# Layer one's operand stored in blocks of 16 tokens, high and low parts in turn, and its 512 columns walked in runs of eight

## The reference, cut to what matters

```python
hs = jnp.concatenate([meta, x], axis=1)          # 16 + 256 tokens
h = rmsnorm(x, gain)
zin = h @ w_in                                    # 2048 x 12288
q, k, v, g_attn, u, g_pool, m_attn, m_pool = jnp.split(zin, cuts, axis=-1)
...                                               # attention over q, k, v; pooled means of u
merged = sigmoid(m_attn) * y_attn + sigmoid(m_pool) * y_pool
return x + merged @ w_out
```

## Time and profile before

| | us |
|---|---|
| median of 3 runs | 2767.71 (2766.85 to 2773.09) |
| the profiled execution | 2766.82 |
| its span in the profile | 2765.1 |
| TensorE busy in the span | 2746.5 (99%) |
| VectorE busy | 1907.3 (69%) |
| ScalarE busy | 1353.2 (49%) |

### The profile page before, as it was taken

The page is one execution under the profiler, slowest core; times in us unless marked ns, Lnnn a source line. Parts: engine busy times, 40 slices in busy tenths (PEclk is TensorE's granted clock), DMA queues, the critical chain, the costliest instruction groups (busy, mean ns, idle before and its releaser), DMA issues.

```text
span 2765.1 us, 39573 instructions
## 1 busy us (share of the span) xinstructions
PE 2746.5 (99%) x16256; PEld 2443.9 (88%) x16256; DVE 1907.3 (69%) x2553; ACT 1353.2 (49%) x1741; POOL 59.4 (2%) x103
## 2 busy tenths in 40 slices
PE   9999999999999999999999999999999999999998
PEld 8899888888888889999999988888888888888887
DVE  7655567778866657888888885566666655666556
ACT  5434654447444436656565643543354443444444
POOL 0000210000000000000000000000000000000000
PEclk9999999999999999999999999999999999999999
DMA  7444445465555454444444445554355455555554
GB/s 273 183 193 158 151 169 197 184 251 184 208 178 211 180 186 168 153 153 153 151 154 151 169 168 212 183 191 163 141 206 197 184 192 204 202 194 191 195 193 152
DMA packets 72852, 506.64 MB, mean 183 GB/s; under 512 B 8384, under 2 KB 8512, under 8 KB 12896
## 3 DMA queue, kind: packets, MB, share of 16 engines
q1 hardware_dynamic: 71136, 497.77, 48.6%
q0 software_dynamic: 1104, 5.90, 0.6%
q10 hardware_dynamic: 432, 0.45, 0.0%
HBM read 499.89 MB, written 2.10 MB: 182 GB/s over the span
## 4 chain that ended last, share of the span: by engine, by line
PE 95%; DVE 3%; ACT 1%; issue 1%; DMA 1%; SPq 0%; DVEq 0%; ACTq 0%
PE double L1399 88%; PE bank L1399 6%; PE bank L1402 1%; DVE wlo L2117 1%; ACT whi L1775 0%; DVE AA L2123 0%; DMA vec<-in_vec 0%; DMA raw<-in_wall 0%; DVE Tn L2625 0%; DVE gz L2117 0%; ACT tmp L1952 0%; DVE ob L2123 0%; DVE acc L2117 0%; ACT L1952 0%; SPq L2920 0%
## 5 line engine op out<-in xcount | busy, mean ns | idle before, releaser
L1399 PE MATMUL double<-AA,whi 128*128 128x512 f32 (+3 forms) x5776 | 1617.0, 348 | 3.3 <-DVE wlo L2117 3.2
L1775 ACT ACTIVATE whi<-raw 128x1024 fp32r<-128x1024 f32 x926 | 926.1, 1050 | 785.2 <-PE double L1399 735.1
L1399 PE MATMUL double<-AA,wlo 128*128 128x256 f32 (+1 forms) x4624 | 1274.9, 276 | 0.0
L2117 DVE TENSOR_TENSOR wlo<-raw,whi 128x1024 fp32r<-128x1024 f32 (+1 forms) x934 | 1100.4, 1214 | 191.8 <-ACT whi L1775 188.7
L1399 PEld LDWEIGHTS double<-AA,whi 128*128 128x128 f32 (+1 forms) x5776 | 1003.9, 188 | 147.3 <-DVE wlo L2117 5.0
L1399 PEld LDWEIGHTS double<-AA,wlo 128*128 128x128 f32 x4624 | 866.7, 187 | 1.0
L1399 PE MATMUL double<-whi,AA 128*128 128x512 f32 x1536 | 481.0, 388 | 0.0
L1399 PEld LDWEIGHTS double<-whi,AA 128*128 128x128 f32 x1536 | 288.1, 188 | 52.7 <-issue 1.9
L1399 PE MATMUL double<-whi,BB 128*128 128x512 f32 x1024 | 309.5, 382 | 0.0
L1399 PE MATMUL double<-wlo,AA 128*128 128x512 f32 x768 | 293.4, 382 | 0.0
L1399 PEld LDWEIGHTS double<-whi,BB 128*128 128x128 f32 x1024 | 191.8, 187 | 33.8
(11 more groups left out here) (334 smaller groups left out, 1688.1 us busy)
## 6 DMA issues: line engine op xcount, KB each, us to landing
raw<-in_wall SPq DMA_DIRECT2D x462, 1024.0 KB, 4.8
raw<-in_wall SPq DMA_DIRECT2D x9, 256.0 KB, 6.4
X<-in_xT SPq DMA_DIRECT2D x1, 2048.0 KB, 11.3
Mm<-in_memT POOLq DMA_DIRECT2D x1, 2048.0 KB, 15.5
tmp<-rqk POOLq DMA_DIRECT2D x16, 128.0 KB, 2.2
mblk<-in_memT SPq DMA_DIRECT2D x8, 256.0 KB, 4.5
dec<-in_dec POOLq DMA_DIRECT2D x1, 1536.0 KB, 8.6
hs<-in_hsT SPq DMA_DIRECT2D x4, 272.0 KB, 5.6
```

Of the source, the lines that this page charges most:

```text
L1399: return q.matmul(out, lhsT, rhs, start=start, stop=stop, skip_group_check=True)
L1775: q.activation(hi_of(j)[:, c], raw[j % RAW][:, c], ACT.Copy).then_inc(S("w_hi"), 1)
L2117: return q.tensor_tensor(out, a, b, o)
```

## The change

The columns of `AA` for one row tile are stored in 17 blocks of 16 tokens, and each block holds its 16 high columns and then its 16 low columns. The view `AL` becomes five-dimensional (row tile, block, high or low, token in block). The first block is the meta tokens', so the 512 columns without it lie one after the other, from column 32 to column 543 (`ALtok`).

- The 512-column matmul of the `META_TAGS` now takes these 512 columns with `leap(…, 4, 8)`. Its result in PSUM has the same order: 16 high, 16 low, and so on.
- The 256-column matmul of the `META_TAGS` takes the high columns only, 16 of every 32, and adds onto the same places in PSUM. With `by_four` it goes in runs of four, with 32 columns (128 bytes) from run to run, in operand and output.
- The matmuls of kind `W` take high or low columns with `by_four`, so 128 bytes from run to run in the operand; their output is walked as before.
- ScalarE and VectorE write `AL` in 17 runs of 16 columns instead of in one run of 272.
- The 28 sums of the `META_TAGS` go through a new `summed_runs`, which adds columns that lie 16 apart instead of 256 apart.

```diff
-    AL = AA[:, :].rearrange("p (k s n) -> p k s n", s=2, n=L)
+    AL = AA[:, :].rearrange("p (k b s e) -> p k b s e", k=NT, s=2, e=META)
+    ALtok = AA[:, :].rearrange("p (k n) -> p k n", k=NT)
...
             if pr["kind"] == "W":
-                return AL[:, a, :, :]
+                return AL[:, a, :, :, :]
             if pr["tag"] in META_TAGS:
-                return AL[:, a, :, META:L]
+                return AL[:, a, 1:, :, :]
...
+        def by_four(x):
+            return x.rearrange("p b (s r) -> p s b r", s=4)
...
-                hh, hl = both[:, 0, :], both[:, 1, :]
+                if kind == "W" or pr["tag"] in META_TAGS:
+                    hh, hl = both[:, :, 0, :], both[:, :, 1, :]
+                else:
+                    hh, hl = both[:, 0, :], both[:, 1, :]
...
                     if kind == "W":
-                        o, hh, hl = (leap(x, 4, 4) for x in (out[:, m * 512:m * 512 + L], both[:, 0, :], both[:, 1, :]))
-                        mm_group(o, wh[:, i, cs], hh, start=first, stop=False)
-                        mm_group(o, wh[:, i, cs], hl, start=False, stop=False)
-                        ins = mm_group(o, wl[:, i, cs], hh, start=False, stop=last)
+                        o, h_, l_ = leap(out[:, m * 512:m * 512 + L], 4, 4), by_four(hh), by_four(hl)
+                        mm_group(o, wh[:, i, cs], h_, start=first, stop=False)
+                        mm_group(o, wh[:, i, cs], l_, start=False, stop=False)
+                        ins = mm_group(o, wl[:, i, cs], h_, start=False, stop=last)
...
                         if pr["tag"] in META_TAGS:
-                            mm_group(o, wh[:, i, c], both, start=first, stop=False)
-                            ins = mm_group(leap(h, 4, 4), wl[:, i, c], leap(hh, 4, 4), start=False, stop=last)
+                            x = ALtok[:, a, 2 * META:2 * L]
+                            high = o.rearrange("p (b s e) -> p b s e", s=2, e=META)[:, :, 0, :]
+                            mm_group(leap(o, 4, 8), wh[:, i, c], leap(x, 4, 8), start=first, stop=False)
+                            ins = mm_group(by_four(high), wl[:, i, c], by_four(hh), start=False, stop=last)
...
-            q.activation(AL[:, k, 0, :], hs[:, k, :], ACT.Copy, scale=V("norm_gain", k)).then_inc(S("a_hi"), 1)
+            q.activation(AL[:, k, :, 0, :], hs[:, k, :].rearrange("p (b e) -> p b e", e=META), ACT.Copy, scale=V("norm_gain", k)).then_inc(S("a_hi"), 1)
...
+        def summed_runs(out, r):
+
+            both = double[r["b"]][:, :].rearrange("p (b x e) -> p b e x", x=2, e=META)
+            q.reduce_sum(flat(out).rearrange("p (b e) -> p b e", e=META), both, mybir.AxisListType.X).then_inc(S("sum"), 1)
+            q.wait_ge(S("sum"), r["sum"])
...
-            stt(AL[:, k, 1, :], hs[:, k, :], V("norm_gain", k), AL[:, k, 0, :].bitcast(F32), ALU.mult, ALU.subtract).then_inc(S("a_lo"), 1)
+            stt(AL[:, k, :, 1, :], hs[:, k, :].rearrange("p (b e) -> p b e", e=META), V("norm_gain", k), AL[:, k, :, 0, :].bitcast(F32), ALU.mult, ALU.subtract).then_inc(S("a_lo"), 1)
```

More of the change, by code:

```diff
@@ L2213, in s_gp @@
             g = flat(gpool[:, 2 * j:2 * j + 2, :])
-            summed(two(g), r)
+            summed_runs(two(g), r)
             tt(two(g), two(g), rx, ALU.mult).then_inc(S("ev"), 1)
@@ L2239, in s_q @@
             x = qT[:, 2 * j:2 * j + 2, :]
-            summed(x, r)
+            summed_runs(x, r)
             stt(x, x, float(128 ** -0.5), rx, ALU.mult, ALU.mult).then_inc(S("ev"), 1)
@@ L2292, in s_ga @@
             x, y = tmps[r["t"]][:, :], tmps[r["t2"]][:, :]
-            summed(two(y), r)
+            summed_runs(two(y), r)
             tt(two(y), two(y), rx, ALU.mult).then_inc(S("ev"), 1)
```

## The result

The change makes the kernel slower: 2794.12 us (median of 4 runs, 2793.47 to 2794.70) against 2768.12 us (4 runs of the kernel before beside it), a ratio of 1.0091 with a 95% interval of 1.0080 to 1.0103. The forecast was 2765.5 us, its range ended at 2771, and the slowest rival stood at 2775.0.

A forecast was written before the change was run, and what follows sets the result against it. The prediction took PE's time per matmul step as the bound. Its terms, -5.5 (512-column), +2.7 (256-column) and +0.6 us (kind W), summed to -2.2 us: 2767.71 - 2.2 = 2765.5 us, range 2760 to 2771 us.

The forecast's parts named there:

- the slowest rival: Wide step of 128 bytes costs in pairs and kind W alike: +7.3 us, 2775.0 us, chance 0.06.
- The bound: Whole kernel: PE runs almost without idle time, so only its time per step counts, and a nanosecond counts in full.
- wrong if: Refuting signs: 512-column record above 394 ns, 256-column one past 280, or a pair of k moving over 0.3 us.
- The 256-column matmul: META_TAGS stages, 896 matmuls going from 64-byte to 128-byte steps: +3 ns each within +1 to +6, +2.7 us.
- the one row that had such a walk: Unit leading into kind N, fours 128 bytes apart: record 280 ns against 275, step 345.6 against 340.0.
- Kind W: 1152 matmuls of 272 columns, only the operand getting the 128-byte step: +0.5 ns each, +0.6 us; bounds -2.1 to +6.9 us.
- The 512-column matmul: META_TAGS stages, 896 matmuls taking wo's walk in eights: -7.6 ns on 512 steps, -4.3 on 384, -5.5 us.
- pace of `q`: 343.3 ns a step, taken for q and mp (384 steps): a gain of 4.3 ns each.
- The third rival: ga's extra 6.6 ns come from the operand's place and stay, leaving only losses: +3.3 us, 2771.0 us, chance 0.12.
- that something is half the size: Argument against the rival blaming operand place: ga and q share a walk yet differ by only 3.3 ns.
- The second rival: Fours 128 bytes apart cost everywhere: pairs +0.4 us, kind W +6.9 us, 2775.0 us, chance 0.06.
- All of layer two unchanged: Sign expected in the profile after: wo and all of layer two stay as they were.

The follow-up runs named there:

- e_entry: Kernel before with the 256-column matmul of the units leading into kind N walked in fours 64 bytes apart instead of 128; 2770.47 us, ratio 1.0006.
- e_low128: Kernel before with only the META_TAGS stages' 256-column matmul walked in fours 128 bytes apart, in operand and output; 2777.01 us, ratio 1.0029.
- e_wo128: Kernel before with only wo's 256-column matmul walked in fours 128 bytes apart; 2771.21 us, ratio 1.0015.
- e_run8: Kernel after, layout kept, with kind W and the 256-column matmul reading in runs of eight, 128 bytes apart, instead of four; 2778.1 us, ratio 1.0034.
- e_out: Kernel before with only the results in PSUM in blocks of 16 high, 16 low, summed by summed_runs; operand and its walk kept; 2767.32 us, ratio 1.0002.
- e_turned: Kernel before with row tiles laid out high 272, low 256, low meta 16: 512 columns walked in eights, high columns keeping 64 bytes; 2769.6 us, ratio 1.0005.
- e_pitch: Kernel before with the row tiles of the operand view used from wo on 2176 bytes apart instead of 2048, walks unchanged; 2811.59 us, ratio 1.0157.
- e_shift: Kernel before with the operand view AT, used from wo on, starting 128 bytes later at its own pitch; 2803.67 us, ratio 1.0125.
- e_shift_both: Kernel before with AT starting 128 bytes later and the weights of the stages reading it shifted by 128 bytes too; 2784.32 us, ratio 1.0055.

## Why the prediction was wrong, point by point

**The bound held.** PE without idle time, no new wait, sums of 1223 ns, writers of `AA` unchanged, `wo` at 87.05 us: a nanosecond per slot did count in full. The signs it named as "wrong if" came true at once: 402 for a limit of 394, 287 for 280, a pair of `k` (a quarter of the stretch) +1.0 us for 0.3.

**The step that failed first is "The 256-column matmul".** It was put at +3 ns within +1 to +6 and measured +10.3 ns, 9.2 us in place of 2.7. The upper bound came from the one row that had such a walk. The text saw that its weights lie at other addresses and concluded that less than 5 ns might be the walk's. It was the other way round: against fours 64 bytes apart the same walk costs about 5 ns a step in such a unit of `f1` (e_entry), +5.1 ns in `ga` at before's addresses (e_low128) and +13.3 ns at `wo`'s (e_wo128). In the kernel after, fours cost +13.1 ns a step over eights at the same 128 bytes (e_run8). A row from other addresses was no bound on either side.

**"Kind W"** was put at +0.5 ns, at most +6, and measured +10.1 in `k` and +9.6 in `v`, 9.9 us in all in place of 0.6. Its reasons were that the output walk stays and that this leaves half the addresses as they were. But in the stages of e_out the output's walk is worth nothing; if that holds for kind `W` too, which no run tried, keeping it saved nothing. And "the whole 6 ns" was the same row's bound carried over. Of the 10.1 ns in `k`, e_run8 gives 6.2 to the runs of four at that step, and 3.9 remain.

**"The 512-column matmul"** was put at -7.6 and -4.3 ns and measured +5.0 in `ga`. The inference "what differs is the walk and the layout", and then all of it to the walk, was wrong: e_turned has the walk and no gain, e_pitch leaves `wo` its walk and takes 4.9 of its 6.6 ns a step. The layout was the cause for these 4.9 ns, by the way row tiles follow on each other; the other 1.7 ns stay open. The second term of this sum rests on a misreading: the "pace of `q`" is that of the last pair of `q`, and `ma`, counted with the pace of `ga`, has such a pair too (343.5 ns). It is a second pace of the same stages and not a property of `q` and `mp`; the sum is 1.3 us smaller by it. The third rival, "The walk was not the cause", said so at 0.12 and was right in that; with the losses at their true size it would have come to 2767.71 + 9.2 + 9.9 = 2786.8 us. The sentence that set it aside ("that something is half the size") compared `ga` with `q`, two stages with one pitch, so it could not show the pitch's effect. The +4.1 us that the 512-column slots lose belong to the 256-column walk beside them: with that in eights they stand at 229.9 ns.

**The second rival, "The wide step costs everywhere",** had the mechanism at 0.06: it passed its own point of decision (4 and 5 ns) by far. Its size, +7.3 us, rested on the same row. The page cited for it, the Trainium skill's "Advanced Engine Details and Errata" (PSUM Cachelines), puts the cost in the output; e_out has two such output walks beside the earlier trace rows, with the same 44.37 us, so here the cost is not there.

**Layer two's +4.3 us** stood in no case. "All of layer two unchanged" holds for its instructions and not for its pace.

**What stays open.** Which resource the reads contend for: no view has it, only that operand walk and operand pitch each move the slot, and the place of operand or weights sometimes. "TensorE: Matmul & The Clock Gate" (Step-by-step: what each phase is for) of the Trainium skill gives the weight load a port of its own. `mv`, which slows from 220.2 to 229.6 ns when only the operand that the weight load reads is shifted (e_shift), is hard to square with a load that never touches the running read. It is no proof, since `f2` slows there too without any change of its own. Also open is what chooses between the two paces of `rv`, of `f2` and of layer one's stages. A pitch of 2304 bytes with constant starts in layer one wasn't tried.

No version here beats the kernel before by more than its interval.

## What to carry to other kernels

Take the price of a walk only from a row with the same operand pitch and the same starts of operand and weights; a row from elsewhere is no ceiling (here the same walk cost 5 to 13 ns a step), and the range must be several times wider. When a layout is changed to give one reader a better walk, price its other readers first: here 2048 matmuls (896 and 1152) paid about 10 ns each for a gain that the wanted walk did not have in this layout. Where two stages differ in walk and place, move one of the two alone, an edited line as in e_pitch, before moving data.

## What the runs showed of the hardware

- The output's walk in PSUM didn't count in the five `META_TAGS` stages: the 512-column output straight or in runs of 16, the 256-column one in fours 64 or 128 bytes apart, gave the same slots to 0.1 ns (e_out: 234.1 and 112.6).
- With fours 128 bytes apart in this layout, `k` took 132.3 ns a matmul for 122.2, and a step of `ga` 361.9 ns for 346.6; in eights at the same places it was 6.2 ns less in `k`, and 13.1 ns less in the step.
- At `wo` the operand's pitch counts and a constant shift does not: row tiles 2176 bytes apart took a step of `wo` from 340.0 to 344.9 ns (e_pitch), a start 128 bytes later left it at 340.1 (e_shift).
- A matmul's slot depends on its neighbour, in both directions: at `wo` the 512-column slot rose by 7.5 ns with the wider walk beside it (e_wo128), in `ga` it fell by 2.9 (e_low128). Only the sum of a step can be compared.
- Some stages have two paces at the full granted clock. In layer two they are 221.9 or 231.2 ns in `rv` and 220 or 231 in `f2`, with unchanged instructions; layer one's stages have 346.6 or 343.4 ns a step. The choice can differ from head to head (e_shift_both), from block to block (`f2` in e_entry), and be set by edits far away (e_shift: `f2` +15.6 us). A pair of `f2` in the kernel before, and in the kernel after:

```profile
2380.21:2390.77 10.56, 10.56 (x50) 1.00 0.64 259
```

```profile
2408.10:2418.66 10.56, 10.56 (x50) 1.00 0.71 267
```

Both are fast at 10.56 us, where e_pitch and e_shift have 11.07. So up to some 16 us of this kernel can appear or vanish in a stage that no edit touches, and a comparison of whole times has to be read beside the stretches.
